# The order of the first mixer in a three-block kernel: projections between the inverse's steps, attention under inverse and scan, and half of its output product in other banks

## The chip, the cores and the metric

The kernel runs on one core of one Trainium2 chip. The metric is device time in microseconds (us); lower is better.

## The reference

The input is 256 tokens of 1024 values, to which 16 meta tokens are added in front. One block with two kinds of mixer comes first, then a layer of differential attention and a layer of stick-breaking attention, each with its MLP. The change touches the first block's mixer alone:

```
u = rms_norm(h, norm_mix_pre)
proj = u @ w_in
dq, dk, dv, dz, db, da, aq, ak, av = split(proj)      # 4 x 512, 8, 8, 512, 128, 128 columns
o_dn = gated_deltanet_group(dq, dk, dv, dz, db, da, conv_w, ...)
o_at = axial_gqa_group(aq, ak, av, q_norm, k_norm)
mix = concat([o_dn, o_at]) @ w_out
h = h + rms_norm(mix, norm_mix_post)

gated_deltanet_group: q, k, v = split(silu(short_conv(concat[dq, dk, dv])))   # 5 taps along the tokens
    q, k = l2_norm(q), l2_norm(k)                     # 4 heads of 128
    per chunk of 64 tokens: uw = triangular_solve(I + A, [v * beta, k * beta * exp(g)]) 
    o = scan over the chunks, once forward and once backward, and their sum
    o = rms_norm(o, o_norm_w) * silu(dz)
axial_gqa_group: rms_norm and rope on q (8 heads of 64) and k (2 heads), softmax(q k^T) v
```

All is computed in float32. A product of an activation with a weight is made of three matmuls of rounded halves: both operands are split into a high and a low part, and low times low is left out.

## The kernel before

**Engines.** Everything is written out by hand: each engine has its own instruction stream and counting semaphores between them. Two lists of steps, `STAGE_1` and `STAGE_2`, give the order of the first mixer. Each engine walks both lists with `in_order`, and runs its own part of each step that it has one for. So moving a name in a list moves the step on TensorE (PE), VectorE (DVE), ScalarE (ACT) and GpSimd (POOL) at once.

**Weights.** SyncE (SP) loads weights in tiles of 1 MB into `RAW`, a ring of three. Each tile holds two halves. ACT writes the high part `WH` of a half (L1219), DVE (L1610) or POOL (L2119, in the first mixer every other half) the low part `WL`. `WH` and `WL` are rings of four halves, and a half is freed once PE has used it. `ahead(n)` is the place in an engine's stream where it splits half n. The three matmuls of `mm3` are L580, L581 and L582. Steps that take a half of weights: `conv.0` to `conv.11` (24 matmuls of 272 columns, 128 channels of dq, dk, dv each), `kv.0` to `kv.3`, `q.0` to `q.4` (with `ba` a few columns at the start), `z.0` to `z.4`, and the output product.

**Steps without weights.** `conv.i`'s taps are four DVE operations (L1731) that read its PSUM bank. `ktok`, `vtok` turn k and v by transposes. `start`, `meta` prepare the chunks. `inv.0` to `inv.14` invert the triangular matrices of all chunks at once; their matmuls are L822, L827 and L832 (128x128), and L842 and L848 (64x64) for `inv.13` and `inv.14`; between two of them stand DVE operations. `solve` (L862) is followed by a chain of small DVE operations (L1828, L1830). `rows.0` to `rows.3` are the norm and the rope of attention's q and k on POOL and DVE. `qp.0` to `qp.2` prepare q for the scan: PE (L929, L937 sums of squares by 128x1 products), DVE (L1879, L1883, L1885), POOL (the square root by a power, L2123), and DVE again (L1918). `in.0`, `in.1` (L949, L959, L960) turn attention's q and k.

**Second list.** `scan.d.i` is step i of the scan in direction d: L974, L988/L989, L996, L1004 and L1012 are its matmuls. `gqa.n` is one of 20 attention pieces: scores of piece n (L1024), the maximum, exponent and reciprocal on DVE and ACT (L1946, L1948, L1953, L1955), transposes of an earlier piece (L1034, L1036), and a product with v of one earlier still (L1045, L1046, L1047). The result goes to `MH`/`ML` 4 to 7. `on.0` to `on.6` are the norm and gate of the scan's result, mostly on POOL (L2292 squares, L2295, L2123 power, L2301, L2304), the transposes (L1059) and `MH`/`ML` 0 to 3. The output product follows: `out_half(n, k)` for k = 0 to 5 (12 matmuls of 512 columns each) and `out_last` for k = 6 and 7, into PSUM banks 0 to 3; then `between` (norm and residual), `features` (transposes into banks 4 to 7) and the MLP. `WROW`, a row buffer, holds z's gate until `on` has used it; then SP loads the norm's row there for `between`.

**PSUM.** Eight banks. The projections use 4 and 5, the inverse 0 to 3, other steps 6 and 7. `keep_warm` (L591) fills PE's pauses at the layer's borders with products that nothing reads.

## Time and profile before

| | us |
|---|---|
| median of 3 runs (lowest to highest) | 1148.88 (1143.24 to 1149.07) |
| profiled execution | 1142.91 |
| its span, from first to last instruction | 1141.1 |
| PE busy in the span | 1077.6 |
| DVE, ACT, POOL busy | 632.9, 555.7, 243.3 |
| mean granted TensorE clock | 0.973 of full |

The profiled execution is one run of its own. Its time stands beside its span, which is 1.8 us shorter, and lies 6.0 us under the median. [...] In the span the first list runs from about 20 to 176 us, the second from 176 to 242 us, the output product from 242 to 263.8 us.

### The profile page before, as it was taken

The page shows a single profiled execution, that of the slowest core. Times are in us where ns is not written, and L with a number is a line of the kernel's source. Part 1 is how long each engine was busy: PE and PEld are TensorE (multiplying, and loading weights), DVE is VectorE, ACT ScalarE, POOL GpSimd, SP SyncE. Part 2 cuts the span into 40 slices and gives each one's busy share as a digit, 9 for nine tenths or more (in the row PEclk, how much of TensorE's full clock was granted, in tenths as well). Part 3 has the DMA queues.
Part 4 walks back from the last instruction along what each step waited for, and adds up shares of the span by engine and source line. Part 5 has one row for each costly group of instructions (what it writes and reads, how often), then busy time and mean ns, then how long its engine had stood idle before and what let it go on. Part 6 is the DMA issues. An engine that isn't in the chain of part 4 may idle for free.

```text
span 1141.1 us, 17631 instructions
## 1 busy us (share of the span) xinstructions
PE 1077.6 (94%) x7367; PEld 966.0 (85%) x7367; DVE 632.9 (55%) x923; ACT 555.7 (49%) x907; POOL 243.3 (21%) x200
## 2 busy tenths in 40 slices
PE   6988998999999999998889999999999999999998
PEld 4977897668999998988668999999899878999997
DVE  4885743636555556167766555546543446554554
ACT  5642332346444545554436444444776656444443
POOL 2522641231000000776351000000332220000000
PEclk8998996999999999999889999999999999999999
DMA  8322200034665565343223565555343324555551
GB/s 256 112 87 98 77 36 0 2 92 134 193 208 184 186 190 198 116 145 121 101 83 125 191 212 185 179 191 186 128 148 111 111 91 146 189 184 187 190 178 73
DMA packets 113951, 160.47 MB, mean 141 GB/s; under 512 B 3776, under 2 KB 97088, under 8 KB 113872
## 3 DMA queue, kind: packets, MB, share of 16 engines
q1 hardware_dynamic: 113872, 159.35, 42.9%
q8 instruction: 58, 0.95, 0.4%
q14 instruction: 21, 0.17, 0.0%
HBM read 158.29 MB, written 1.05 MB: 140 GB/s over the span
## 4 chain that ended last, share of the span: by engine, by line
PE 82%; DVE 9%; ACT 4%; issue 2%; POOL 2%; DMA 0%; SPq 0%; DVEq 0%; POOLq 0%; ACTq 0%
PE PS L580 23%; PE PS L582 22%; PE PS L581 22%; ACT SCR L1219 3%; DVE SCR L1731 1%; PE PS L607 1%; DVE SCR L2048 1%; POOL SM L2123 1%; PE PS L1180 1%; DVE H L1657 1%; PE PS L1203 1%; PE PS L974 1%; PE PS L1104 1%; PE PS L827 1%; PE PS L822 1%
## 5 line engine op out<-in xcount | busy, mean ns | idle before, releaser
L1219 ACT ACTIVATE WH<-RAW 128x1024 fp32r<-128x1024 f32 (+1 forms) x291 | 304.1, 1054 | 247.2 <-PE PS L582 247.0
L1610 DVE TENSOR_TENSOR WL<-RAW,WH 128x1024 fp32r<-128x1024 f32 x226 | 282.9, 1259 | 233.3 <-ACT WH L1219 233.3
L580 PE MATMUL PS<-UH,WH 128*128 128x256 f32 (+2 forms) x1128 | 318.9, 283 | 3.5 <-POOL WL L2119 3.4
L582 PE MATMUL PS<-UH,WL 128*128 128x256 f32 (+2 forms) x1128 | 318.6, 282 | 0.0
L581 PE MATMUL PS<-UL,WH 128*128 128x256 f32 (+2 forms) x1128 | 318.5, 282 | 0.0
L580 PEld LDWEIGHTS PS<-UH,WH 128*128 128x128 f32 (+1 forms) x1128 | 212.4, 188 | 6.6 <-POOL WL L2119 3.5
L581 PEld LDWEIGHTS PS<-UL,WH 128*128 128x128 f32 (+1 forms) x1128 | 211.7, 188 | 1.8
L582 PEld LDWEIGHTS PS<-UH,WL 128*128 128x128 f32 (+1 forms) x1128 | 212.7, 189 | 0.6
L2119 POOL TENSOR_TENSOR WL<-RAW,WH 128x1024 fp32r<-128x1024 f32 (+1 forms) x65 | 155.5, 2402 | 210.6 <-ACT WH L1219 210.6
L580 PE MATMUL PS<-WH,MH 128*128 128x512 f32 (+1 forms) x464 | 177.4, 382 | 5.3 <-DVE ML L2054 3.0
L581 PE MATMUL PS<-WL,MH 128*128 128x512 f32 (+1 forms) x464 | 175.5, 378 | 0.0
L582 PE MATMUL PS<-WH,ML 128*128 128x512 f32 (+1 forms) x464 | 175.0, 377 | 0.0
L1219 ACT ACTIVATE SCR<-PS 128x512 f32<-128x512 f32 (+7 forms) x199 | 95.5, 506 | 150.5 <-PE PS L582 71.2
L2123 POOL TENSOR_TENSOR SM<-SM 128x1 f32<-128x1 f32 (+6 forms) x34 | 30.0, 882 | 590.9 <-DVE SM L1621 577.2
L580 PEld LDWEIGHTS PS<-WH,MH 128*128 128x128 f32 x464 | 88.3, 190 | 22.9 <-issue 8.2
L582 PEld LDWEIGHTS PS<-WH,ML 128*128 128x128 f32 x464 | 88.3, 190 | 16.4
L581 PEld LDWEIGHTS PS<-WL,MH 128*128 128x128 f32 x464 | 88.1, 190 | 14.1
L580 PE MATMUL PS<-WH,UH 128*128 128x256 f32 (+2 forms) x248 | 77.5, 312 | 4.7 <-DVE SCR L1731 4.7
L581 PE MATMUL PS<-WL,UH 128*128 128x256 f32 (+2 forms) x248 | 75.5, 304 | 0.0
L582 PE MATMUL PS<-WH,UL 128*128 128x256 f32 (+2 forms) x248 | 75.3, 304 | 0.0
L580 PEld LDWEIGHTS PS<-WH,UH 128*128 128x128 f32 (+1 forms) x248 | 48.3, 195 | 6.9 <-DVE SCR L1731 4.8
L1219 ACT ACTIVATE MH<-SCR 128x512 fp32r<-128x512 f32 (+1 forms) x41 | 25.2, 616 | 53.8 <-DVE SCR L1677 53.8
(286 smaller groups left out, 1257.3 us busy)
## 6 DMA issues: line engine op xcount, KB each, us to landing
RAW<-in_gu SPq DMA_DIRECT2D x44, 1024.0 KB, 5.1
RAW<-in_dn SPq DMA_DIRECT2D x22, 1024.0 KB, 4.9
RAW<-in_w_up SPq DMA_DIRECT2D x16, 1024.0 KB, 5.8
RAW<-in_w_down SPq DMA_DIRECT2D x16, 1024.0 KB, 4.9
...
```

The lines of the kernel that those rows point to most:

```text
L580: e.matmul(o, lh, rh, start=start, stop=False)
L581: e.matmul(o, lh, rl, start=False, stop=False)
L582: return e.matmul(o, ll, rh, start=False, stop=stop)
L607: ins = e.transpose(PS[:, b, o + 128 * c:o + 128 * c + 128], XN[:, c, 128 * k:128 * k + 128], idn)
L822: ins = e.matmul(v[:, h, :], MT[:, h, :], X[:, h, :], start=True, stop=True)
L827: ins = e.matmul(v[:, h, :], XT[:, h, :], T0[:, h, :], start=True, stop=True)
L974: ins = e.matmul(v0[:, h, :], T0[:, h, :], X[:, h, :], start=True, stop=True)
L1104: ins = e.matmul(PS[:, 4 + i, 0:nk], QTT[64 * i:64 * i + 64, h, 128 * c:128 * c + 128], KTT[64 * i:64 * i + 64, h, 0:nk], start=True, stop ...
L1219: return e.activation(o, i, func, bias=bias, scale=scale, accum_out=acc)
L1610: e.tensor_tensor(half_view(WL, n_), half_src(n_), half_view(WH, n_).bitcast(F32), SUB).then_inc(s_lo_dve, 1)
L2119: e.tensor_tensor(half_view(WL, n_), half_src(n_), half_view(WH, n_).bitcast(F32), SUB).then_inc(s_lo_pool, 1)
L2123: e.tensor_tensor(o, x, s, POW).then_inc(*done)
```

## The change

The diff, cut to its core:

```diff
 STAGE_1 = steps_of(
-    "ba gates.0 conv.0 conv.1 gates.1 conv.2 gates.2 conv.3 gates.3 silu.0 conv.4 conv.5 ktok.0 conv.6 ktok.1 conv.7 "
-    "start.0 start.1 meta.0 silu.1 kv.0 kv.1 inv.0 kv.2 kv.3 inv.1 meta.1 vtok.0 q.0 q.1 solve vtok.1 q.2 q.3 inv.2 "
-    "inv.3 meta.2 vtok.2 q.4 conv.8 inv.4 rows.0 conv.9 inv.5 meta.3 conv.10 inv.6 rows.1 conv.11 silu.2 inv.7 meta.4 "
-    "z.0 z.1 inv.8 rows.2 z.2 z.3 inv.9 meta.5 z.4 rows.3 inv.10 meta.6 inv.11 inv.12 qp.0 inv.13 qp.1 inv.14 qp.2 "
-    "in.0 in.1")
+    "ba gates.0 conv.0 conv.1 gates.1 conv.2 gates.2 conv.3 gates.3 silu.0 kv.0 kv.1 ktok.0 ktok.1 kv.2 kv.3 start.0 start.1 "
+    "meta.0 q.0 q.1 inv.0 meta.1 q.2 inv.1 q.3 q.4 rows.0 z.0 solve z.1 z.2 z.3 z.4 inv.2 inv.3 meta.2 conv.4 inv.4 conv.5 "
+    "inv.5 meta.3 conv.6 inv.6 rows.1 conv.7 silu.1 inv.7 meta.4 conv.8 inv.8 vtok.0 conv.9 inv.9 vtok.1 vtok.2 rows.2 "
+    "meta.5 conv.10 inv.10 meta.6 rows.3 conv.11 silu.2 inv.11 in.0 in.1 inv.12 gqa.0 qp.0 inv.13 gqa.1 qp.1 inv.14 gqa.2 "
+    "qp.2 gqa.3")
 STAGE_2 = steps_of(
-    " ".join(f"scan.0.{i} scan.1.{i} gqa.{i}" for i in range(8)) +
-    " on.0 gqa.8 on.1 gqa.9 on.2 gqa.10 gqa.11 on.3 gqa.12 on.4 gqa.13 gqa.14 gqa.15 gqa.16 gqa.17 on.5 gqa.18 on.6 gqa.19")
+    " ".join(f"scan.0.{i} gqa.{2 * i + 4} scan.1.{i} gqa.{2 * i + 5}" for i in range(8)) +
+    " on.0 og.4 on.1 og.5 on.2 og.6 on.3 og.7 on.4 on.5 on.6")
...
         w_cols("ba", win, 2048, 16)
-        for b in (2, 3, 4, 5):
+        for b in (2, 3):
             w_cols(("conv", b), win, 256 * b, 256)
         w_rows("kv", win, 0, 8, 2576, 256)
         for k in range(2):
             w_rows(("q", k), win, 4 * k, 4, 2064, 512)
-        for b in (0, 1):
-            w_cols(("conv", b), win, 256 * b, 256)
         for k in range(2):
             w_rows(("z", k), win, 4 * k, 4, 1536, 512)
-        for k in range(4):
+        for b in (4, 5, 0, 1):
+            w_cols(("conv", b), win, 256 * b, 256)
+        for k in (2, 3, 0, 1):
             w_rows(("out", 1, k), A["w_out"], 2 * k, 2, 0, 1024)
...
+        QSQ = SCR[:, at[0] - 1024:at[0]].rearrange("p (a b) -> p a b", a=4)
...
-        TA, TB = PB[0][:, 0:256], PB[1][:, 0:256]
+        TA, TB, TK = (O[i // 2].rearrange("p a b -> p (a b)")[:, 256 * (i % 2):256 * (i % 2) + 256] for i in range(3))
...
+        SUMS = [4 if r == 1 else 0 for r in range(7)]
+        TURN = [0 if r == 1 else 4 for r in range(6)]
...
-                return mm3(PS[:, 2 * c + m, :], MH[:, k, t], ML[:, k, t], wh[:, 0, s], wl[:, 0, s], start, stop)
+                return mm3(PS[:, SUMS[r] + 2 * c + m, :], MH[:, k, t], ML[:, k, t], wh[:, 0, s], wl[:, 0, s], start, stop)
...
+            def og(k):
+                out_half(1, half_of(("out", 1, k // 2), k % 2), k, mix_ready(1, k), k == 4)
+
...
-            in_order(STAGE_2, dict(scan=scan, gqa=gqa, on=on))
-            for k in range(6):
-                out_half(half_of(("out", 1, k // 2), k % 2), k, mix_ready(1, k), k == 0)
-            out_last(1, [half_of(("out", 1, 3), j) for j in range(2)], [6, 7], [mix_ready(1, 6), mix_ready(1, 7)])
+            in_order(STAGE_2, dict(scan=scan, gqa=gqa, on=on, og=og))
+            for k in range(2):
+                out_half(1, half_of(("out", 1, 0), k), k, mix_ready(1, k), False)
+            out_last(1, [half_of(("out", 1, 1), j) for j in range(2)], [2, 3], [mix_ready(1, 2), mix_ready(1, 3)])
...
             def gqa_in(i):
                 if i == 0:
-                    ac.wait_ge(*qp_p["n"])
...
-                    dv.wait_ge(*vt_v[2])
...
+            def og(k):
+                ahead(half_of(("out", 1, k // 2), k % 2))
+
...
-                    po.wait_ge(*me_a["s", 1])
-                    e.tensor_tensor(QTG, CV[:, 0:4, 16:272], CV[:, 0:4, 16:272], MUL).then_inc(*qp_o.step("sq"))
+                    po.wait_ge(*gr_v[1, 1, "s2"])
+                    po.wait_ge(*gr_o[1, 1, "s2"])
+                    e.tensor_tensor(QSQ, CV[:, 0:4, 16:272], CV[:, 0:4, 16:272], MUL).then_inc(*qp_o.step("sq"))
```

In words. Of the convolution's projections only dk's four now come ahead of `kv`, `q` and `z`; the other eight stand between the steps of the inverse. Attention begins already in the first list, and its pieces alternate with the scan's steps. The output product begins with attention's own half, k = 4 to 7 (`og`), between the steps of `on`; k = 0 to 3 follow. It sums into banks 4 to 7, and the `features` that follow use banks 0 to 3. The weights come in the order of their new use. Some temporaries have moved to other buffers, so that three waits fall away. PE does the same products as before.

The change adds four lines ahead of `mm3` and some later: L580 to L582 of before are L584 to L586 of the changed kernel, PE's L842, L848, L929, L937, L974, L1024, L1034, L1036 are L846, L852, L933, L941, L978, L1028, L1038, L1040, L988/L989 are L992/L993, DVE's L1879, L1883, L1885, L1918, L1946, L1948, L1953, L1955 are L1887, L1891, L1893, L1925, L1953, L1955, L1960, L1962, and POOL's L2119, L2123, L2292, L2295, L2301, L2304 are L2129, L2133, L2305, L2308, L2314, L2317.

PE's stream from the last inverse steps to the first scan steps, before (L832 is `inv.12`, L929 `qp.0` and `qp.1`, L842 and L848 `inv.13` and `inv.14`, L937 `qp.2`, L949 to L960 `in.0` and `in.1`, L974 the scan, L1024 attention's scores):

```order
L832 MATMUL PS<-CST,SCR 128x128 x16
L929 MATMUL PS<-SCR 128x128 x4
L842 MATMUL PS<-SCR 64x64 x16
L929 MATMUL PS<-SCR 128x128 x4
L848 MATMUL PS<-SCR 64x64 x16
L937 MATMUL PS<-CST,SCR 128x1 x8
L949 MATMUL PS<-CST,SCR 128x128 x8
...
L974 MATMUL PS<-SCR 128x128 x8
L1024 MATMUL PS<-SCR 128x272
L974 MATMUL PS<-SCR 128x128 x8
L1024 MATMUL PS<-SCR 128x272
L988 MATMUL PS<-SCR 128x128
```

The same place in the changed kernel; `in.0` and `in.1` now stand ahead of it:

```order
L836 MATMUL PS<-CST,SCR 128x128 x16
L1028 MATMUL PS<-SCR 128x272
L933 MATMUL PS<-SCR 128x128 x4
L846 MATMUL PS<-SCR 64x64 x16
...
L1028 MATMUL PS<-SCR 128x272
L941 MATMUL PS<-CST,SCR 128x1 x8
L1028 MATMUL PS<-SCR 128x272
L1038 MATMUL PS<-CST,SCR 128x128 x2
L1040 MATMUL PS<-CST,SCR 16x128
L978 MATMUL PS<-SCR 128x128 x4
L1028 MATMUL PS<-SCR 128x272
```

What moved: `in.0` and `in.1` no longer lie between `qp.2` and the scan's first step; two scores (L1028) and the transposes of one piece do, and scores and the scan's products now alternate by four.

DVE's stream at the same place, before (L1879 to L1918 belong to `qp.2` and the scan's first step, L1946 and L1948 to attention):

```order
L1879 TENSOR_SCALAR SM<-PS 128x2x4
L1883 TENSOR_SCALAR SM<-SM 128x2x4
L1885 TENSOR_TENSOR SM<-SM 128x8
L1918 TENSOR_TENSOR SCR<-SCR,SM 128x512
L1946 TENSOR_REDUCE SM<-PS 128x1
```

And in the changed kernel:

```order
L1887 TENSOR_SCALAR SM<-PS 128x2x4
L1891 TENSOR_SCALAR SM<-SM 128x2x4
L1893 TENSOR_TENSOR SM<-SM 128x8
L1953 TENSOR_REDUCE SM<-PS 128x1
L1955 TENSOR_SCALAR SM<-SM 128x1
L1960 RECIPROCAL SM<-SM 128x1
L1962 TENSOR_SCALAR SCR<-SCR,SM 128x272
L1925 TENSOR_TENSOR SCR<-SCR,SM 128x512
```

What moved: four operations of an attention piece now stand between `qp.2`'s last scalar (L1893) and the operand of the scan's first step (L1925).

POOL's stream around `on`, before (L2292 to L2304 are `on`, L2119 the low parts of the output product's and the MLP's weights):

```order
L2292 TENSOR_TENSOR SCR<-SCR 128x512 x2
L2295 TENSOR_SCALAR SM<-SM 128x8
L2123 TENSOR_TENSOR SM<-SM 128x8
L2301 TENSOR_TENSOR SCR<-SCR,SM 128x512
L2304 TENSOR_TENSOR SCR<-SCR,WROW 128x512
L2301 TENSOR_TENSOR SCR<-SCR,SM 128x512
L2304 TENSOR_TENSOR SCR<-SCR,WROW 128x512
L2119 TENSOR_TENSOR WL<-RAW,WH 128x1024 x4
```

And in the changed kernel:

```order
L2305 TENSOR_TENSOR SCR<-SCR 128x512
L2129 TENSOR_TENSOR WL<-RAW,WH 128x1024
L2305 TENSOR_TENSOR SCR<-SCR 128x512
L2308 TENSOR_SCALAR SM<-SM 128x8
L2133 TENSOR_TENSOR SM<-SM 128x8
L2129 TENSOR_TENSOR WL<-RAW,WH 128x1024
L2314 TENSOR_TENSOR SCR<-SCR,SM 128x512
L2317 TENSOR_TENSOR SCR<-SCR,WROW 128x512
L2314 TENSOR_TENSOR SCR<-SCR,SM 128x512
L2317 TENSOR_TENSOR SCR<-SCR,WROW 128x512
```

What moved: two low parts (halves 26 and 28) now stand inside the chain of `on`, where none stood before.

## Rows read from the trace of the kernel before

**Rows 1.** The page: busy time of the engines, share of the span

```profile
PE 1077.6 (94%) x7367; PEld 966.0 (85%) x7367; DVE 632.9 (55%) x923; ACT 555.7 (49%) x907; POOL 243.3 (21%) x200
```

**Rows 2.** Windows (us, busy of PE, PEld, DVE, ACT, POOL, clock, DMA share, GB/s)

```profile
44.00:264.00 220.00, 202.42 (x1324) 167.44 (x1323) 124.17 (x272) 82.69 (x170) 82.23 (x74) 0.92 0.19 61
...
65.00:69.00 4.00, 4.00 (x22) 4.00 (x23) 3.96 (x14) 1.17 (x2) 0.64 (x1) 0.57 0.00 0
...
89.00:96.00 7.00, 4.79 (x14) 3.92 (x15) 2.79 (x10) 0.00 (x0) 0.00 (x0) 0.51 0.43 145
...
167.70:191.60 23.90, 22.18 (x89) 17.52 (x89) 4.95 (x10) 6.71 (x13) 6.18 (x5) 0.50 0.00 0
191.60:242.00 50.40, 45.86 (x259) 29.05 (x258) 30.34 (x93) 16.11 (x51) 11.09 (x10) 1.00 0.03 11
242.00:264.00 22.00, 22.00 (x99) 18.23 (x99) 6.68 (x9) 10.06 (x15) 10.15 (x5) 1.00 0.49 149
```

**Rows 3.** What PE waited for from 44 to 264 us: total, times, longest

```profile
PE PS L580 <- DVE SCR L1731: 4.7, 1, 4.7
PE PS L774 <- DVE SCR L1828: 4.0, 1, 4.0
PE PS L1004 <- DVE SCR L1930: 1.9, 2, 1.0
...
PE PS L974 <- issue: 1.4, 1, 1.4
```

**Rows 4.** PE in order of time, 166 to 192 us: start, us, operation

```profile
166.51 2.52 PE L937 MATMUL PS<-CST,SCR 128*128 128x1 f32 x16
...
182.46 3.76 PE L974 MATMUL PS<-SCR 128*128 128x128 f32 x16 [1.37 <-issue]
...
187.35 0.79 PE L988 MATMUL PS<-SCR 128*128 128x128 f32 x2
```

**Rows 5.** DVE in order of time: a convolution's taps; then 168 to 176 us

```profile
43.14 2.10 DVE L1731 SCALAR_TENSOR_TENSOR SCR<-PS,COLS,SCR 128x270 f32<-128x270 f32 x4 [0.25 <-ACT SCR L1219]
...
169.06 0.17 DVE L1879 TENSOR_SCALAR SM<-PS 128x8 f32<-128x8 f32 x1 [2.98 <-PE PS L937]
170.99 1.00 DVE L1883 TENSOR_SCALAR SM<-SM 128x8 f32<-128x8 f32 x1 [1.76 <-POOL SM L2123]
172.02 0.96 DVE L1885 TENSOR_TENSOR SM<-SM 128x8 f32<-128x8 f32 x1
172.91 0.68 DVE L1918 TENSOR_TENSOR SCR<-SCR,SM 128x512 f32<-128x512 f32 x1
```

**Rows 6.** DVE, one attention piece at 224 us

```profile
223.82 0.44 DVE L1946 TENSOR_REDUCE SM<-PS 128x1 f32<-128x272 f32 x1
...
224.56 0.36 DVE L1955 TENSOR_SCALAR SCR<-SCR,SM 128x272 f32<-128x272 f32 x1
```

**Rows 7.** POOL in order of time: `rows.0`, `qp.2`, `on` and a low part

```profile
113.61 2.91 POOL L2123 TENSOR_TENSOR SM<-SM 128x16 f32<-128x16 f32 x1
...
120.47 2.37 POOL L2119 TENSOR_TENSOR WL<-RAW,WH 128x1024 fp32r<-128x1024 f32 x1
...
169.31 1.65 POOL L2123 TENSOR_TENSOR SM<-SM 128x8 f32<-128x8 f32 x1 [8.01 <-DVE SM L1879]
170.92 1.04 POOL L2281 TENSOR_TENSOR SCR<-SCR,SM 128x512 f32<-128x512 f32 x1
...
216.13 2.10 POOL L2292 TENSOR_TENSOR SCR<-SCR 128x512 f32<-128x512 f32 x2 [1.43 <-DVE SCR L1939]
...
222.77 1.64 POOL L2123 TENSOR_TENSOR SM<-SM 128x8 f32<-128x8 f32 x1
...
227.04 1.04 POOL L2301 TENSOR_TENSOR SCR<-SCR,SM 128x512 f32<-128x512 f32 x1 [2.63 <-DVE SM L1973]
228.16 1.29 POOL L2304 TENSOR_TENSOR SCR<-SCR,WROW 128x512 f32<-128x512 f32 x1
```

**Rows 8.** PE by line, 217 to 234 us, attention alone: busy, mean ns

```profile
L1024 PE MATMUL PS<-SCR 64*128 64x272 f32 x16 | 5.8, 441 | 0.0
```

More of the change, by code:

```diff
@@ L670, in out_last @@
                 for b in range(4):
-                    emptied[b] = mixed[b // 2][r, b % 2]
+                    emptied[SUMS[r] + b] = mixed[b // 2][r, b % 2]
             def mlp(r, u):
@@ L1466, in on @@
                         act(MH[:, h, :], PS[:, h, 0:256], ACT.Copy).then_inc(*mx_hi.step((1, h)))
-            in_order(STAGE_1, dict(ba=ba, gates=gates, conv=conv, silu=silu, kv=kv, q=q, z=z, ktok=ktok, start=start, inv=inv, meta=meta,
+            in_order(STAGE_1, dict(gqa=gqa, ba=ba, gates=gates, conv=conv, silu=silu, kv=kv, q=q, z=z, ktok=ktok, start=start, inv=inv, meta=meta,
                                **{"in": gqa_in}))
-            in_order(STAGE_2, dict(scan=scan, gqa=gqa, on=on))
-            for k in range(7):
+            in_order(STAGE_2, dict(scan=scan, gqa=gqa, on=on, og=og))
+            for k in range(3):
                 ahead(half_of(("out", 1, k // 2), k % 2))
@@ L1960, in gqa, with og @@
                                            ).then_inc(*mg_lo.step(j))
+            def og(k):
+                ahead(half_of(("out", 1, k // 2), k % 2))
             def on(i):
@@ L1978, in on @@
                                                ).then_inc(*mx_lo.step((1, h)))
-            in_order(STAGE_1, dict(ba=ba, gates=gates, conv=conv, kv=kv, q=q, z=z, ktok=ktok, vtok=vtok, start=start, inv=inv, meta=meta,
+            in_order(STAGE_1, dict(gqa=gqa, ba=ba, gates=gates, conv=conv, kv=kv, q=q, z=z, ktok=ktok, vtok=vtok, start=start, inv=inv, meta=meta,
                                solve=solve, qp=qp, rows=rows))
-            in_order(STAGE_2, dict(scan=scan, gqa=gqa, on=on))
-            for k in range(7):
+            in_order(STAGE_2, dict(scan=scan, gqa=gqa, on=on, og=og))
+            for k in range(3):
                 ahead(half_of(("out", 1, k // 2), k % 2))
@@ L2286, in scan, with og @@
                     e.tensor_tensor(O[c], O[c], grp[d, c][4], ADD).then_inc(*sc_o[d].step("o"))
+            def og(k):
+                ahead(half_of(("out", 1, k // 2), k % 2))
             def on(i):
@@ L2306, in _ @@
             in_order(STAGE_1, dict(ba=ba, gates=gates, conv=conv, kv=kv, q=q, z=z, ktok=ktok, meta=meta, qp=qp, rows=rows))
-            in_order(STAGE_2, dict(scan=scan, on=on))
-            ahead(half_of(("out", 1, 3)))
+            in_order(STAGE_2, dict(scan=scan, on=on, og=og))
+            ahead(half_of(("out", 1, 1)))
             between(1)
```

44 lines of the change are left out of this document (21 added, 23 removed).

## The prediction, on record before the changed kernel ran

> **What bounds the kernel now.** I read the page first: PE is busy in 94% of the span, every other engine in 55% or less [rows 1]. So a stretch of the kernel lasts as long as PE's own work at the clock that it is granted, plus what PE waits. The products stay the same, so the change can only move those two. Then I read windows around what moves, 44 to 264 us: PE busy 202.4 of 220 us, clock 0.92 [rows 2]. That leaves two stores:
>
> - Waiting: 220.0 - 202.4 = 17.6 us. The chain of waits names 4.7 us at `kv.0` behind a convolution's taps, 4.0 us at L774 behind the small DVE operations after `solve`, 1.9 us in the scan (twice), 1.4 us at the scan's second step [rows 3]. The rest, 5.6 us, is small.
> - [...] 65 to 69 us, right behind the 4.7 us wait, has a mean of 0.57 over 4 us: about 3.4 us at half, of which half, 1.7 us, is lost. 89 to 96 us, around the 4.0 us wait, has 4.79 us of busy time at 0.51: 2.4 us lost. 167.7 to 191.6 us has 22.18 us of busy time at 0.50: 11.1 us lost [rows 2]. Together 15.2 us.
>
> The third piece has no long wait in front. It begins with the thinnest PE work of the stage, the 64x64 products of `inv.13` and `inv.14` and `qp.2`'s 128x1 products, of which 16 rows take 2.52 us [rows 4]. It ends only inside the unbroken run of L988/L989 that begins at 187.35 us [rows 4].
>
> **The change part by part.** I walked PE's new stream with the durations of before, full clock where it was full.
>
> *Work.* The same products, no term. The output product is 96 matmuls in 21.8 us, whichever banks and order they take; a bank's number has no row of its own and no reason for a price. The loads are the same tiles in another order. DMA's share is 0.19 in this stretch [rows 2], so a tile is there when its half is split.
>
> *Waits that go.* `kv.0` now stands right behind `conv.3`, whose four taps take 2.10 us [rows 5]. From PE's end of `conv.3` to the taps' end 1.15 us stay of 4.7. The chain after `solve` takes 4 us on DVE as before, but `z.1` to `z.4`, 4 x 2.8 us of products, now lie between: the 4.0 us go. The 1.4 us at the scan's second step is replaced below.
>
> *Waits that come.* (1) `z.0` waits some 0.65 us (an estimate, one ACT copy) until `q.4`'s bank is free. (2) `z.3` takes half 14, an even one, whose low part is POOL's, and POOL has `rows.0` in front of it (the norm's square root alone 2.91 us, the low part 2.37 us [rows 7]). By my walk it is ready 2.9 us after PE wants it. (3) By the walk 0.3 us at `inv.3` and 0.9 us at `meta.5` behind `vtok.2`. (4) Ahead of the scan's first step stands what `qp.2` needs: L1879 0.17, POOL's power 1.65, L1883 1.00, L1885 0.96, then four operations of piece 3 that stand between (1.10 us from 223.82 to 224.92 in a piece like it [rows 6]), then L1918 0.68 [rows 5, 7]: 5.6 us. Before, `in.0` and `in.1` lay in between, and L1918, begun at 172.91, was done well before the scan at 176 us. Now two scores and the transposes of one piece lie there, about 1.2 us. PE waits 4.3 us (4.0 to 4.6 by how the ends fall). (5) In the scan 1.9 us as before. (6) Behind the scan POOL is the long pole: squares 2.10, a power of 1.64 with a short scalar ahead, two products per half of 1.04 and 1.29, so 4.7 [rows 7], two low parts that now stand between, 4.8, and 1.7 us for the crossings to DVE and back: 15.1 us from the last attention piece to the gated result. `og.4` to `og.7`, 48 matmuls, cover half of the product's 21.8, 10.9 us. PE waits 4.2 us, and 0.3 for the transposes. Before, twelve attention pieces stood between `on`'s steps and covered this. (7) Small ones I set at 1.2 us, against 5.6 before, since attention and scan now alternate and each has work of the other behind which to hide.
> Sum: 1.15 + 0.65 + 2.9 + 1.2 + 4.3 + 1.9 + 4.5 + 1.2 = 17.8 us, against 17.6. The waits pay nothing, they only change places.
>
> *Clock.* All hangs on it. With no half clock anywhere the stretch would be 15.2 - 0.2 = 15.0 us shorter. But every pause of 4 us or more in this stretch had half clock around it [rows 2, 3]. The new pauses are 2.9 us before `z.3`, 4.3 us before the scan, 4.2 us before the last half of the product. For the first and the last I take what the old ones cost, 1.7 and 2.4, less a little for the shorter one: 1.6 + 2.4 = 4.0 us. For the middle one I take a fall for certain: `inv.13`, `inv.14` and `qp.2` are still there, now with a pause right behind them.
> How long it stays down is the unknown. Bound from below: the old pauses were over after 3.4 and 6.8 us, with dense work behind them. Bound from above: the old third piece lasted 23.9 us, over scan products and scores [rows 2]. Now behind the pause come scan products of four with attention's scores, transposes and products with v between. From 191.6 us on, the same kinds of products held full clock over 50.4 us, though PE waited 4.5 of them [rows 2]. But from 182.46 to 187.35 us scan products and scores at half clock did not raise it, and L988/L989 did [rows 4]. I take 8 us of busy time at half, nearer the short end, since the mix is richer than the one that failed: 4.0 us lost.
>
> [...] At 170.99 us L1883 and L1885, 128x8 elements each, took 1.00 and 0.96 us beside POOL's L2281 of 1.04 us, while L1879 of the same size took 0.17 alone [rows 5, 7]. [...]
>
> **Sum.** Clock and waits -15.0, side pauses +4.0, middle +4.0: -7.0 us. Against the profiled execution that is 1142.9 - 7.0 = 1135.9 us. The runs shown have a median 6.0 us above it, so I say 1148.9 - 7.0 = 1141.9 us. Outside the stretch nothing moves: the norm's row for `between` is loaded when `on` is done with its buffer, and 10.9 us of product lie between.
>
> **The rivals.** A change of under about 0.5%, 5.7 us, can't be told from none.
>
> - A, my forecast (0.40): as summed. By the side pauses (0 to 4 us) and the length at half it lies between -12 and -2 us: 1137 to 1147.
> - B, the clock comes back only in the scan's L988/L989, as before (0.24). Up to those lie 13.1 us of work at full clock, which then cost twice: 32 scan products, 3.8 us (16 took 3.76 at half [rows 4]), and four and a half attention pieces at 2.1 us, 9.3 (two rows of L1024 are a piece, so eight pieces took 17 us [rows 8]). -15.0 + 4.0 + 13.1 = +2: 1151. For it: 182.46 to 187.35 us. Against it: attention's transposes and 256-column products were not in that mix.
> - C, the other side (0.16): attention now also splits the run of L988/L989 in groups of eight, so the very thing that raised the clock is gone, and half clock goes on into the rest of the second list. Of the 45.9 us that PE was busy from 191.6 to 242 us [rows 2] some 10 are done by then, so 36 us are left; half to most of it slow, 17 to 30 us, gives, with B's +2, +19 to +32: 1168 to 1181. It decides if 8 us or more of work behind the first L992 still run at half. Against it: 191.6 to 242 us at full clock with waits [rows 2]. For it: that stretch never had to climb, it only had to stay up.
> - D, no fall in the middle and none at the sides (0.10): the scores among `inv.12` to `qp.2` make that place dense enough. -15.0: 1134. Against it the pause of 4.3 us.
> - E, a wait that I don't see (0.10): low parts, loads or ring slots that come late because an engine's order now puts them behind something, such as (2) or (6) longer by 5 us or more. With A that gives about -2 to +8, say 1152.
>
> **How the numbers follow.** The likeliest is A, 1141.9 us. The range 1132 to 1163 takes in A, B, D and E and leaves out C, 0.16, and a few hundredths below D. Signs are mixed: A's own range is 1137 to 1147. Faster by over 0.5%: A 0.27, D 0.10, B 0.03, in all 0.40. Within 0.5%: A 0.13, B 0.14, E 0.06, in all 0.33. Slower: B 0.07, C 0.16, E 0.04, in all 0.27.
>
> **What would show it.** In the profile after: PE's waits at `kv.0` about 1 us, none at L774 after `solve`, one near 3 us in the `z` steps on POOL's low part, one near 4 us on L1925 before the first L978, one near 4 us between `og.7` and the transposes of `on`. Windows from the pause on show how long 0.50 lasts: some 8 us is A, until the first L992 is B, far past it C, none is D. I would be wrong if the pause before the scan were under 2 us (then D), if the half clock began already in the `inv` steps and went through to the scan, or if the wait for `on` were 8 us or more, because the two low parts come late from SP's loads.

## The result, and the profile after

The changed kernel takes 1157.33 us (median of 4 runs, 1155.65 to 1157.61), the kernel before, timed beside it, 1148.95 us. The ratio is 1.0085 with a 95% interval of 1.0057 to 1.0114: slower, by 8.4 us in the medians. Forecast were 1141.9 us and a gain. The time lies inside the stated range of 1132 to 1163 us, but on the other side of the kernel before. The profiled execution took 1157.22 us, 14.3 us more than that of before. The kernel before has executions near 1143.5 and near 1148.8 us, and its profile is one of the first kind; the median beside the changed kernel, 1148.95 us, comes from three of the second kind and one of the first. In the later timings most were of the first kind (medians of 1143.7 to 1144.5 us), so the loss is nearer 13 us against those.

The page and windows over the stretch that the change touches, to compare with [rows 1, 2] (columns as there). The first window is the stretch, the others are those in which the profile grants half clock, 0.50 of full:

```profile
PE 1085.7 (94%) x7367; PEld 971.7 (84%) x7367; DVE 649.2 (56%) x923; ACT 555.2 (48%) x907; POOL 244.6 (21%) x200
```

```profile
44.00:280.00 236.00, 211.67 (x1333) 174.04 (x1332) 141.70 (x273) 83.23 (x172) 83.62 (x74) 0.88 0.18 58
79.30:86.10 6.80, 6.80 (x28) 6.22 (x28) 2.54 (x7) 0.00 (x0) 5.08 (x5) 0.50 0.01 2
96.40:103.20 6.80, 6.24 (x33) 5.46 (x34) 3.08 (x5) 3.48 (x6) 1.57 (x2) 0.50 0.24 85
144.20:147.60 3.40, 3.40 (x16) 3.40 (x17) 3.33 (x7) 0.00 (x0) 3.17 (x6) 0.50 0.51 133
178.30:209.00 30.70, 25.25 (x81) 16.53 (x81) 9.63 (x26) 6.83 (x19) 4.76 (x5) 0.50 0.00 1
263.60:270.50 6.90, 6.22 (x18) 5.13 (x19) 1.70 (x4) 2.48 (x5) 3.00 (x2) 0.51 0.24 77
```

PE is idle for 236.0 - 211.7 = 24.3 us, against 17.6. It is busy at half clock for 47.9 us, so half clock costs 24.0 us, against 15.2. Together 15.5 us more. The output product ends at 278.96 us, before at 263.84: 15.1 us later. So the whole loss lies in this stretch, to within 0.8 us at the end of the span, and it is 6.7 us of waiting and 8.8 us of clock.

What PE waited for there, to compare with [rows 3]:

```profile
PE PS L978 <- DVE SCR L1925: 5.6, 1, 5.6
PE PS L1063 <- POOL SCR L2317: 5.5, 2, 3.5
PE PS L817 <- DVE SCR L1817: 3.8, 2, 3.2
PE PS L866 <- DVE SCR L1812: 2.9, 1, 2.9
PE PS L1008 <- DVE SCR L1937: 1.8, 2, 0.9
PE PS L913 <- DVE SCR L1780: 1.3, 1, 1.3
```

The old waits of 4.7 and 4.0 us are gone. In their place stand one before the scan's first step (L978), one before `on`'s transposes (L1063), and two in the inverse: `solve` (L866) and `inv.3` (L817).

PE around the scan's start, in order of time, to compare with [rows 4]:

```profile
177.92 0.27 PE L1040 MATMUL PS<-CST,SCR 128*16 128x128 f32 x1
183.75 2.05 PE L978 MATMUL PS<-SCR 128*128 128x128 f32 x8 [5.56 <-DVE SCR L1925]
...
205.16 0.80 PE L992 MATMUL PS<-SCR 128*128 128x128 f32 x2
...
209.96 0.39 PE L992 MATMUL PS<-SCR 128*128 128x128 f32 x2
```

The clock falls at 178.3 us. The wait has then lasted 0.1 us (L1040 ends at 178.19), so it is not the wait that brought the clock down. Ahead of it stand `inv.13`, `inv.14` and `qp.2`'s 128x1 products. Eight rows of scan products then take 2.05 us, not the 1.06 us that they take at full clock (e5). The clock comes back only inside the first unbroken run of L992/L993, at 209.0 us: two rows of them take 0.80 us at 205.16 and 0.39 us at 209.96.

DVE's chain ahead of the scan, against [rows 5], and three places before it:

```profile
65.53 4.70 DVE L1854 TENSOR_TENSOR SCR<-SCR,CST 16x64 f32<-16x64 f32 x1 [0.37 <-POOL SCR L2222]
...
70.40 0.20 DVE L1854 TENSOR_TENSOR SCR<-SCR,CST 16x64 f32<-16x64 f32 x1
...
87.02 2.05 DVE L1838 TENSOR_TENSOR SCR<-SCR 128x96 f32<-128x96 f32 x1
...
94.59 4.62 DVE L1817 TENSOR_TENSOR SCR<-SCR,CST 128x512 f32<-128x512 f32 x4
...
177.10 0.17 DVE L1887 TENSOR_SCALAR SM<-PS 128x8 f32<-128x8 f32 x1 [0.78 <-PE PS L941]
179.03 1.00 DVE L1891 TENSOR_SCALAR SM<-SM 128x8 f32<-128x8 f32 x1 [1.76 <-POOL SM L2133]
...
182.08 1.52 DVE L1925 TENSOR_TENSOR SCR<-SCR,SM 128x512 f32<-128x512 f32 x1
```

POOL at the same times, against [rows 7]:

```profile
65.40 4.75 POOL L2129 TENSOR_TENSOR WL<-RAW,WH 128x1024 fp32r<-128x1024 f32 x2
...
86.52 4.80 POOL L2129 TENSOR_TENSOR WL<-RAW,WH 128x1024 fp32r<-128x1024 f32 x2
...
93.90 3.56 POOL L2207 TENSOR_TENSOR WROW<-WROW,ROWS 128x512 f32<-128x512 f32 x2 [2.58 <-ACT WROW L1226]
```

L1854 reads 16x64 elements. It takes 0.20 us alone and 4.70 us when it meets two low parts of POOL in a row that last 4.75 together. L1838 on 128x96 takes 2.05 us next to a low part; the same operation takes 0.26 us next to nothing in the kernel before, where it is L1830. The four L1817 take 4.62 us, against 2.49 in the kernel before; what runs beside them is L2207, not a low part.

### The profile page after: what moved, and what is told of

Its sections match the earlier page's. It is cut to its first block, busy times and chain, and to the rows that moved or that the text cites. A ratio compares the mean times of both kernels' runs of the same rounds, so it can differ in the third digit from the quotient of the medians.

```text
span 1155.4 us, 17635 instructions
## 1 busy us (share of the span) xinstructions
PE 1085.7 (94%) x7367; PEld 971.7 (84%) x7367; DVE 649.2 (56%) x923; ACT 555.2 (48%) x907; POOL 244.6 (21%) x200
## 4 chain that ended last, share of the span: by engine, by line
PE 79%; DVE 10%; ACT 4%; issue 3%; POOL 3%; DMA 0%; SPq 0%; DVEq 0%; POOLq 0%; ACTq 0%
PE PS L584 22%; PE PS L586 21%; PE PS L585 21%; ACT SCR L1226 3%; POOL SM L2133 1%; PE PS L611 1%; DVE SCR L2058 1%; PE PS L826 1%; PE PS L1187 1%; PE PS L1028 1%; POOL WL L2129 1%; DVE H L1665 1%; DVE SCR L1739 1%; PE PS L1210 1%; PE PS L978 1%
## 5 line engine op out<-in xcount | busy, mean ns | idle before, releaser
L584 PE MATMUL PS<-UH,WH 128*128 128x256 f32 (+2 forms) x1128 | 320.3, 284 | 3.5 <-POOL WL L2129 3.4
L586 PE MATMUL PS<-UH,WL 128*128 128x256 f32 (+2 forms) x1128 | 319.8, 284 | 0.0
L584 PEld LDWEIGHTS PS<-UH,WH 128*128 128x128 f32 (+1 forms) x1128 | 213.6, 189 | 6.3 <-POOL WL L2129 3.5
L586 PEld LDWEIGHTS PS<-UH,WL 128*128 128x128 f32 (+1 forms) x1128 | 213.8, 190 | 0.6
L2129 POOL TENSOR_TENSOR WL<-RAW,WH 128x1024 fp32r<-128x1024 f32 (+1 forms) x65 | 155.1, 2397 | 194.1 <-ACT WH L1226 194.1
L584 PE MATMUL PS<-WH,MH 128*128 128x512 f32 (+1 forms) x464 | 178.7, 385 | 5.3 <-DVE ML L2064 3.0
L586 PE MATMUL PS<-WH,ML 128*128 128x512 f32 (+1 forms) x464 | 175.5, 378 | 0.0
L1226 ACT ACTIVATE SCR<-PS 128x512 f32<-128x512 f32 (+8 forms) x199 | 95.2, 507 | 160.6 <-PE PS L586 72.8
L2133 POOL TENSOR_TENSOR SM<-SM 128x1 f32<-128x1 f32 (+6 forms) x34 | 30.0, 883 | 596.1 <-DVE SM L1629 576.9
L584 PEld LDWEIGHTS PS<-WH,MH 128*128 128x128 f32 x464 | 88.7, 191 | 23.1 <-issue 8.2
L586 PEld LDWEIGHTS PS<-WH,ML 128*128 128x128 f32 x464 | 88.6, 191 | 16.7
L584 PE MATMUL PS<-WH,UH 128*128 128x256 f32 (+2 forms) x248 | 76.2, 307 | 1.8 <-DVE SCR L1739 1.0
L586 PE MATMUL PS<-WH,UL 128*128 128x256 f32 (+2 forms) x248 | 74.1, 299 | 0.0
L584 PEld LDWEIGHTS PS<-WH,UH 128*128 128x128 f32 (+1 forms) x248 | 47.2, 190 | 4.4 <-issue 1.5
```

Of the source, the lines that this page charges most:

```text
L584: e.matmul(o, lh, rh, start=start, stop=False)
L586: return e.matmul(o, ll, rh, start=False, stop=stop)
L1226: return e.activation(o, i, func, bias=bias, scale=scale, accum_out=acc)
L2129: e.tensor_tensor(half_view(WL, n_), half_src(n_), half_view(WH, n_).bitcast(F32), SUB).then_inc(s_lo_pool, 1)
L2133: e.tensor_tensor(o, x, s, POW).then_inc(*done)
```

## The experiments

The experiments change the order of steps, who makes a low part, or add warming products (`keep_warm`, read by nobody; "filler" below) where PE waits. "Idle" and "lost" are sums over PE's stretch from 44 us to the end of the output product, from the profiled execution of each run. "Lost" is half of PE's busy time at half clock.

| kernel | median us | ratio to before, 95% | product ends | idle | lost |
|---|---|---|---|---|---|
| before | 1148.95 | | 263.8 | 17.6 | 15.2 |
| changed | 1157.33 | 1.0057 to 1.0114 | 279.0 | 24.3 | 24.0 |
| e1 `qp` early | 1157.43 | 1.0044 to 1.0129 | 269.8 | 19.8 | 19.6 |
| e2 44 warming products | 1153.15 | 1.0043 to 1.0103 | 271.8 | 17.9 | 12.8 |
| e3 low parts of `on` by DVE | 1155.69 | 1.0054 to 1.0108 | 276.8 | 22.5 | 22.6 |
| e4 low parts of q, z by DVE | 1154.02 | 1.0018 to 1.0094 | 278.3 | 22.2 | 24.8 |
| e5 20 warming products | 1144.22 | 0.9987 to 1.0031 | 268.0 | 18.9 | 12.0 |
| e6 projections' order alone | 1145.40 | 0.9993 to 1.0043 | 265.4 | 14.8 | 19.9 |
| e7 attention under `on` | 1154.43 | 1.0051 to 1.0156 | 277.2 | 21.9 | 24.2 |
| e8 three edits | 1142.59 | 0.9962 to 1.0040 | 264.3 | 15.0 | 13.3 |
| e9 before, 12 warming products | 1146.85 | 1.0013 to 1.0034 | 265.6 | 17.1 | 14.5 |
| e10 e8 and two more fillers | 1138.96 | 0.9933 to 0.9967 | 260.6 | 11.2 | 6.8 |
| e11 e8 with `qp` early | 1146.93 | 1.0002 to 1.0033 | 268.3 | 18.7 | 15.9 |

The kernel before was timed anew beside each group: 1144.49 us for e1 to e4, 1144.05 for e5 to e8, 1143.70 for e9 to e11. Its executions lie in separate groups, and the ratio is not simply the quotient of two medians. Besides the two groups named above, five of its 71 later executions took 1132.3 to 1133.3 us, at a mean clock of 0.981 to 0.983 instead of 0.971. That is 11 us less, which is what its half clock from 167.7 to 191.6 us costs (11.1 us); no trace of such an execution was kept, so where their clock stayed up is not shown. The changed kernel was timed in the first round alone, in four executions, so "under the changed kernel" compares two rounds of timing; the kernel before has its groups at the same times in all of them.

Warming products count as busy, so they are not in "idle"; the part of them at half clock is in "lost".

**e1: does the wait before the scan bring the clock down?**

```diff
-    "... in.0 in.1 inv.12 gqa.0 qp.0 inv.13 gqa.1 qp.1 inv.14 gqa.2 qp.2 gqa.3"
+    "... in.0 in.1 inv.12 qp.0 qp.1 qp.2 gqa.0 inv.13 gqa.1 inv.14 gqa.2 gqa.3"
```

> The changed kernel with qp.0, qp.1 and qp.2 ahead of inv.13, so that DVE and POOL prepare the scan's operand under inv.13, inv.14 and attention pieces 0 to 3. Both theories: PE's wait of 5.6 us for L1925 before the scan shrinks to 1 us or less. Theory pause (the wait makes the clock fall): the half clock from 178 to 209 us is gone or short, so 5 us of wait and 8 to 12 us of clock come off: about 13 to 17 us under the changed kernel, near 1142. Rival thin products (inv.13, inv.14 and qp.2 make it fall whether PE waits or not, as at 167.7 us in the kernel before, which had no wait): half clock still begins near 175 to 180 us and lasts until the scan's L992, only about 4 to 6 us come off, near 1152.

The wait shrank to 0.85 us as expected. The clock fell all the same. PE in order of time:

```profile
169.21 2.13 PE L941 MATMUL PS<-CST,SCR 128*128 128x1 f32 x16 [0.58 <-DVE SCR L1884]
...
176.90 3.30 PE L852 MATMUL PS<-SCR 64*64 64x64 f32 x32
...
184.70 2.05 PE L978 MATMUL PS<-SCR 128*128 128x128 f32 x8 [0.85 <-DVE SCR L1925]
...
187.88 0.69 PE L1038 MATMUL PS<-CST,SCR 128*128 128x128 f32 x2
...
191.46 0.44 PE L1038 MATMUL PS<-CST,SCR 128*128 128x128 f32 x2
...
199.33 0.49 PE L992 MATMUL PS<-SCR 128*128 128x128 f32 x2
```

`inv.14` took 3.30 us, against 1.90 in the changed kernel: half clock began at 170.8 us, in `qp.2`, with no wait ahead of it longer than 0.58 us. It ended at 191.2 us, eight microseconds ahead of the first L992, after 6.5 us of scan products and scores (L1038 takes 0.69 us before and 0.44 us after). So half clock need not last until the L992. The ten executions fall into two groups, four at 1146 to 1150 us and six at 1157 to 1160. The profile is of the first group; the six have a lower mean clock (0.961 to 0.963 against 0.968 to 0.974), and where they lose it is not shown. The rival is right on the fall, which here had thin products and no wait longer than 0.58 us ahead of it, but not on its end. The theory that the wait makes the clock fall fell.

**e2 and e5: the wait stays, but PE has something to do in it.** e2 has 44 for the 20.

```diff
                 if i < 2:
...
+                    if (d, i) == (0, 0):
+                        keep_warm(20, b0)
                     pe.wait_ge(*(sc_o[1] if d else sc_v[0])["t", i])
```

> The changed kernel with 44 warming products (128x128, read by nobody) into bank 0 ahead of the scan's first step, where PE waits 5.6 us; the wait for L1925 itself stays. Theory pause: PE stays busy there, the clock stays at 1.00 until the on steps, 25.3 us of busy time at half become 12.6: about 12 us under the changed kernel, near 1145. Rival thin products: the clock falls anyway before or in the filler, which then takes up to 10 us: same or up to 5 us slower than the changed kernel, 1157 to 1162.

> As the run with 44 warming products ahead of the scan's first step, with 20 instead. There the 44 took 11.6 us, since each leaves two rows of 0.13 us, so they outlasted the 5.6 us wait by 6 us; 20 take about 5.3 us. Theory pause: half clock there is 3 to 7 us long at most instead of 31, and PE loses nothing to the filler: 9 to 12 us under the changed kernel, near 1147. Rival (it was the sheer length of the 44 that brought the clock back, 20 are too few): half clock lasts until the scan's L992 as in the changed kernel, and the time is 1156 to 1158.

e2 took the half clock from 30.7 to 3.4 us (177.3 to 180.7). But 44 products leave 88 rows in the trace, and they lasted 11.62 us, 6 us past the wait. I had sized them by a row each. Its time, 4.2 us under the changed kernel, lies between the two forecasts. e5 in order of time, and its windows after the filler's start:

```profile
179.32 6.26 PE L595 MATMUL PS<-CST 128*128 128x128 f32 x40
185.42 1.06 PE L980 MATMUL PS<-SCR 128*128 128x128 f32 x8
```

```profile
179.70:183.20 3.50, 3.50 (x20) 3.50 (x19) 2.78 (x6) 0.00 (x0) 3.50 (x4) 0.51 0.00 0
183.20:251.40 68.20, 62.44 (x362) 44.64 (x361) 39.09 (x87) 21.14 (x54) 15.03 (x12) 1.00 0.08 21
```

The clock fell although PE had no pause any more, 0.4 us into the filler, and was back 3.4 us later; then 68 us of the very mix of scan and attention ran at full clock. All ten executions lie between 1143.0 and 1145.9 us, 13.1 us under the changed kernel by the medians, by one edit in one place. So the mix can hold full clock. Climbing to it is less sure: in the changed kernel 21 us of the mix, from 183.75 us to the first L992, did not do it, in e1 6.5 us did.

**e3 and e7: the wait for `on`.** e3 takes POOL's two low parts out of the chain, e7 puts attention over it.

```diff
-            on_pool.append(bool(share) and n % share == 0)
+            on_pool.append(bool(share) and n % share == 0 and n not in (26, 28))
```

> The changed kernel with the low parts of halves 26 and 28, which stand inside POOL's chain of on, made by DVE. POOL's chain gets 4.8 us shorter, DVE gets 2.4 us more. Theory port and queue (the two low parts delay the gated result, by their own length and by holding up L1979 and L1983 2.35 us each): PE's waits for L2317, 5.5 us together, fall to 1 us or less, and the half clock from 263.6 to 270.5 us goes: 5 to 9 us under the changed kernel, near 1150. Rival (DVE takes over the delay, since it also has the row sums of on): the wait moves to a DVE line and less than 2 us come off.

```diff
-    " ".join(f"scan.0.{i} gqa.{2 * i + 4} scan.1.{i} gqa.{2 * i + 5}" for i in range(8)) +
-    " on.0 og.4 on.1 og.5 on.2 og.6 on.3 og.7 on.4 on.5 on.6")
+    " ".join(f"scan.0.{i} gqa.{2 * i + 4} scan.1.{i} gqa.{2 * i + 5}" for i in range(6)) +
+    " scan.0.6 gqa.16 scan.1.6 scan.0.7 scan.1.7 on.0 gqa.17 on.1 gqa.18 on.2 gqa.19 og.4 on.3 og.5 og.6 on.4 og.7 on.5 on.6")
```

> The changed kernel with attention pieces 17 to 19 behind on.0, on.1 and on.2, ahead of og.4, so that on's POOL chain starts earlier against PE's work: 5 to 6 us of attention now lie under it. Theory (PE waits since only 10.9 us of product cover a chain of over 15 us): the waits for L2317, 5.5 us, fall to 1 us or less and the half clock of 6.8 us there goes: 5 to 8 us under the changed kernel, near 1151. Rival (DVE and ACT do these pieces late, and POOL waits for DVE's sums behind them): the chain ends later by as much, less than 2 us come off.

e3: the wait for L2317 fell from 5.5 to 3.1 us and the half clock there from 6.9 to 3.4 us, 1.6 us by the medians. e7: 5.5 to 1.3 us, but its half clock of 6.8 us stayed (now at 247.5), 2.9 us by the medians. e7's theory is right on the wait and wrong on the clock. e3's, 1 us or less of wait and 5 to 9 us of time, is wrong in size on both; its rival's "less than 2 us" fits, though no wait moved to a DVE line. The chain in the changed kernel and in e3, DVE in order of time:

```profile
248.90 2.35 DVE L1979 TENSOR_TENSOR SM<-SM 128x4 f32<-128x4 f32 x1
...
256.17 2.35 DVE L1983 TENSOR_TENSOR SM<-SM 128x4 f32<-128x4 f32 x1 [2.05 <-POOL SM L2133]
```

```profile
251.58 0.17 DVE L1979 TENSOR_TENSOR SM<-SM 128x4 f32<-128x4 f32 x1
...
256.55 0.17 DVE L1983 TENSOR_TENSOR SM<-SM 128x4 f32<-128x4 f32 x1 [0.19 <-POOL SM L2133]
```

Four elements a row take 2.35 us beside a low part of POOL (2.39 us) and 0.17 us without. The other direction is there too, in e3: POOL's L2317, 1.26 us by itself, began 0.01 us after a low part of DVE of 1.23 us and took 2.35.

```profile
257.92 2.35 POOL L2317 TENSOR_TENSOR SCR<-SCR,WROW 128x512 f32<-128x512 f32 x1
```

So e3 took 4.8 us out of POOL's chain and gave some of it back.

**e4: the same for q's and z's low parts.** The edit is e3's with the set (8, 10, 12, 14).

> The changed kernel with the low parts of halves 8, 10, 12 and 14 (q's and z's) made by DVE instead of POOL. Theory port (DVE operations with two SBUF inputs are held up for the length of POOL's low part): L1854 (16x64, 4.70 us) and the two L1838 of 2.05 us fall to about 0.3 us, DVE is 8 us less held up and 5 us more busy; the wait of 2.9 us before solve and some of the 3.8 us before inv.2's transposes go, and with them half clock at 79 and 96 us: 3 to 9 us under the changed kernel. Rival (these lengths are not from POOL): L1854 and L1838 stay as long, DVE has 5 us more in a stretch where it is busy 98%, and the kernel gets 2 to 5 us slower.

```profile
67.44 0.21 DVE L1854 TENSOR_TENSOR SCR<-SCR,CST 16x64 f32<-16x64 f32 x1 [0.37 <-POOL SCR L2222]
...
88.89 2.05 DVE L1838 TENSOR_TENSOR SCR<-SCR 128x48 f32<-128x48 f32 x1
```

L1854 fell from 4.70 to 0.21 us and the wait before `solve` from 2.9 to 0.7 us; one L1838 still met a low part, of half 16. The wait at `inv.3` stayed (3.6 us for 3.8), with the four L1817 still at 4.64 us beside L2207. The time didn't follow clearly: idle 2.2 us less, lost 0.8 us more, and of the six executions three took 1147.2 to 1151.5 us and three, the profiled one among them, 1156.6 to 1158.5. So it is shown that POOL's operation holds up DVE's; what that is worth to the whole kernel is not.

**e6: the projections' new order alone.** The first list ends as before, the second is the old one, and the product stands whole behind it.

```diff
-    "... silu.2 inv.11 in.0 in.1 inv.12 gqa.0 qp.0 inv.13 gqa.1 qp.1 inv.14 gqa.2 qp.2 gqa.3"
+    "... silu.2 inv.11 inv.12 qp.0 inv.13 qp.1 inv.14 qp.2 in.0 in.1"
...
-    " ".join(f"scan.0.{i} gqa.{2 * i + 4} scan.1.{i} gqa.{2 * i + 5}" for i in range(8)) +
-    " on.0 og.4 on.1 og.5 on.2 og.6 on.3 og.7 on.4 on.5 on.6")
+    " ".join(f"scan.0.{i} scan.1.{i} gqa.{i}" for i in range(8)) +
+    " on.0 gqa.8 on.1 gqa.9 on.2 gqa.10 gqa.11 on.3 gqa.12 on.4 gqa.13 gqa.14 gqa.15 gqa.16 gqa.17 on.5 gqa.18 on.6 gqa.19"
+    " og.4 og.5 og.6 og.7")
```

> One part of the change alone: the projections between the inverse's steps (and the new load order and buffers), but attention after the inverse and in the old second list, in.0 and in.1 behind qp.2 again, and the whole output product behind the last attention piece, in banks 4 to 7. Theory (attention's new place and the early half of the product cost the time, the projections' order nothing or a little): no wait for L1925 before the scan, none for L2317, half clock near 168 to 192 us as in the kernel before, so 13 to 16 us under the changed kernel, 1141 to 1146, level with before. Rival (the projections' new order costs by itself: waits of 2.9 and 3.8 us at solve and inv.2 and their half clock): 1148 to 1153.

1145.40 us, 11.9 us under the changed kernel and level with before (ratio 0.9993 to 1.0043), as the theory had it. Idle time is 2.8 us less than before, 14.8, and the clock takes it back, 19.9 us lost. Attention's new place and the early half of the product cost the rest; the two are not told apart. Where the clock went I had not foreseen: 3.4 us behind `qp.2`, then 20.5 us in the middle of attention, with one wait of 0.42 us at its start. The first of these ended in `in.0` and `in.1`, the very products over which the kernel before stayed at half clock.

```profile
170.90:174.30 3.40, 3.40 (x14) 2.23 (x14) 1.85 (x2) 1.19 (x2) 3.40 (x3) 0.50 0.00 0
222.10:242.60 20.50, 19.32 (x52) 8.72 (x51) 6.02 (x21) 5.85 (x19) 3.31 (x3) 0.50 0.00 0
```

**e8, e10 and e11: together.** e8 is e5, e7 and e3 in one. e10 adds a filler in each of the two waits in the inverse. e11 is e8 with e1's order and 12 warming products behind `qp.2`, none before the scan.

```diff
             def solve():
...
+                keep_warm(12, 6)
                 for m in iv_v:
                     pe.wait_ge(*m["nc"])
...
                     if i == 3:
+                        if j == 0:
+                            keep_warm(13, 0)
                         pe.wait_ge(*V["e"])
```

> Three edits together: 20 warming products ahead of the scan's first step, attention pieces 17 to 19 under on, and the low parts of halves 26 and 28 made by DVE. If each takes away its own wait and its own half clock, they add up: 10 + 6 us under the changed kernel, 1140 to 1143, at or a little under the kernel before. If a clock that is saved in one place is lost in the next (the short filler leaves it down, or the clock falls elsewhere), 1147 to 1152.

> The combined kernel (20 warming products before the scan, pieces 17 to 19 under on, low parts 26 and 28 by DVE) with 12 warming products more in the 2.9 us wait ahead of solve and 13 in the 3.2 us wait ahead of inv.3. Theory pause for the sides too (half clock at 80 to 87 and 97 to 104 us comes from these waits, 6.5 us lost): 4 to 6 us under the combined kernel, near 1137, under the kernel before. Rival (the clock falls there by the thin work around it, 16x16 products and solve's, filler or not, and the filler outlasts the waits): the same as the combined kernel or up to 4 us slower.

> The combined kernel without the 20 warming products before the scan, but with qp.0, qp.1 and qp.2 ahead of inv.13, and 12 warming products right behind qp.2's. The wait for L1925 (5.6 us) is then hidden under real work, and the filler answers the thin products. Theory: if dense products hold the clock over inv.13 and inv.14, 3 us of wait less the filler's 3: 1 to 4 us under the combined kernel. Rival (inv.13, inv.14 and four scores behind the filler are thin enough to let it fall again, as in the run with qp.2 early): half clock of some 20 us until L992, 5 to 12 us above the combined kernel, and two groups of times.

e8: 1142.59 us, inside the forecast for edits that add up, but only 1.6 us under e5: 14.7 us under the changed kernel, where the three gave 17.6 us one by one. e10: 1138.96 us, ratio 0.9933 to 0.9967: a little faster than the kernel before, and 18.4 us under the changed one. All its executions lie above the five of 1132 to 1133 us that the kernel before had in other rounds. It is 3.6 us under e8, with 4 to 6 forecast. Its windows with half clock, and a wait that is new:

```profile
90.10:93.50 3.40, 3.40 (x10) 2.63 (x9) 3.26 (x6) 0.00 (x0) 1.65 (x1) 0.50 0.88 285
175.40:178.90 3.50, 3.50 (x19) 3.50 (x18) 2.75 (x6) 0.00 (x0) 3.50 (x4) 0.51 0.02 5
233.50:240.30 6.80, 6.80 (x17) 4.77 (x17) 1.72 (x3) 1.48 (x3) 3.62 (x3) 0.50 0.26 58
```

```profile
PE PS L584 <- POOL WL L2134: 1.9, 1, 1.9
```

The two pieces of half clock at 80 and 97 us, 13.6 us in e8, are gone, and so is that at 145 us; one of 3.4 us is new, behind the new wait. So at 80 and 97 us filler in the wait did keep the clock up.

e11: 1146.93 us, 4.3 us above e8. Half clock began at 171.5 us with the filler, and full clock held from 174.9 to 185.2 us, over `inv.13` and `inv.14`. But the filler's 4.47 us stood outside a wait, and 2.2 us of the wait before the scan were left: on DVE L1926, the L1925 of this kernel, stands behind the last two attention pieces and began only at 185.44, 11 us after `qp.2`'s last scalar. At 185.2 us the clock fell again. It was back at 192.0 us, again in the mix and 8.5 us ahead of the first L993, the L992 of this kernel. The rival was nearer on the time, but its 20 us of half clock and its two groups of times did not come. PE and DVE in e11, in order of time:

```profile
189.44 0.69 PE L1039 MATMUL PS<-CST,SCR 128*128 128x128 f32 x2
...
191.98 0.72 PE L1029 MATMUL PS<-SCR 64*128 64x272 f32 x2
```

```profile
173.76 0.17 DVE L1892 TENSOR_SCALAR SM<-SM 128x8 f32<-128x8 f32 x1 [1.76 <-POOL SM L2134]
173.97 0.17 DVE L1894 TENSOR_TENSOR SM<-SM 128x8 f32<-128x8 f32 x1
```

The last two are the L1891 and L1893 of the changed kernel. POOL had nothing beside them here, and they took 0.17 us each, not 1.00 and 0.96.

**e9: the same filler in the kernel before**, ahead of its scan, 12 products.

> The kernel before with 12 warming products (24 rows) ahead of the scan's first step, where it has no wait but half clock since 167.7 us, until the dense L988/L989 raise it at 191.6. Theory (dense 128x128 products in one run raise the clock, wherever they stand): the filler takes 3 to 5.6 us, the clock is back at the latest 7 us after it begins, and 7 to 8 us of the 11.1 that half clock costs come back: 2 to 5 us under the kernel before in the executions in which the clock had fallen. Rival (only a pause's end lets the clock rise, or the scan's thin mix takes it down again at once): 3 to 6 us slower than the kernel before.

```profile
176.59 5.43 PE L591 MATMUL PS<-CST 128*128 128x128 f32 x24
...
188.43 0.49 PE L990 MATMUL PS<-SCR 128*128 128x128 f32 x2
...
192.85 1.16 PE L998 MATMUL PS<-SCR 128*128 128x128 f32 x8
```

The same products as that last row, in the kernel before:

```profile
193.78 1.16 PE L996 MATMUL PS<-SCR 128*128 128x128 f32 x8
```

The clock was back at 181.8 us, 5.2 us into the filler and 10 us earlier than before, so here dense products did raise it. The filler stood in no wait and took 5.43 us, and the clock gave more than that back: at L998 PE was 0.9 us ahead of the kernel before. Then 6.8 us of half clock appeared at 236.5 us, where the kernel before had none, and at the product's end PE was 1.8 us behind. 1146.85 us, 2.3 per mille over before, within 2 us in all twelve executions. The theory's 2 to 5 us of gain did not come, and the loss does not lie where the filler stands. The rival's 3 to 6 us of loss fits the time, but not its mechanism: the clock did rise on filler without a pause, and the scan did not take it down again. Whether the filler brought about the later fall is not shown; e6 lost the clock in the same part of attention without any filler.

## Why the prediction was wrong

The waits were sought in the right places, and the place of the risk, the clock behind the wait before the scan, was named. The step that failed is the choice of its length: "I take 8 us of busy time at half, nearer the short end, since the mix is richer than the one that failed: 4.0 us lost". It was 25.3 us, 12.6 lost. That is rival B's mechanism (0.24): half clock until the scan's L992. Its price, 13.1 us, was right within a microsecond; its time, 1151 us, was not, since the side pauses and the waits came on top. The evidence for it was the row at hand, scan products and scores that had not raised the clock from 182 to 187 us. I weighed against it that the same mix had held full clock later. e5 shows that the mix holds full clock for 68 us, the changed kernel that it need not climb to it in 21 us. Nor is the opposite a rule: in e1 and e11 the same mix did climb, 6.5 and 5.7 us after the scan's start. So 8 us was not an impossible length; what was missing was a reason to put it before 25 us, and the only row that I had on climbing spoke for the long one. The prediction also took the fall for a matter of the pause in part. The fall comes 0.1 us into the pause, and in e1 and e5 without one; what lay ahead of it each time was `qp.2` and its surroundings, which it named too.

Point by point, in the terms of the sum:

- Side pauses, "1.6 + 2.4 = 4.0 us": 11.3 us, from four pieces (6.8 + 6.2 + 3.4 + 6.2 of busy time). The second cause of the miss, 7.3 us. The pieces at 79 and 96 us stand at waits that I had at zero and at 0.3, and went in e10 with filler in those waits. That at 144 us stands behind 16x16 products and a wait of 1.3 us.
- Waits, 17.8 us forecast, 24.3 measured. `kv.0` 1.0 for 1.15, scan 1.8 for 1.9, `meta.5` 1.3 for 0.9, an ACT copy at `z.0` 0.8 for 0.65: right.
- Wait (2), 2.9 us at `z.3` behind POOL's low part: not there. PE came late to it by then, through the wait at `solve` and half clock. In e10, where both are gone, it is there with 1.9 us.
- Wait at `solve`, none forecast, 2.9 us; wait at `inv.3`, 0.3 forecast, 3.8 us. Both end on DVE, and DVE was held up: L1854 by 4.5 us, two L1838 by 1.8 each, four L1817 by some 2 us together. e4 shows it for the first wait, which fell to 0.7 us; for the second it is argued. The prediction had a first sign of it, L1883 and L1885 at 1.00 and 0.96 us beside POOL's L2281, and its sum has no term for it. The traces show how long such operations, with two SBUF inputs, were held up, L1854 for 4.70 us beside 4.75 of POOL and L1979 for 2.35 beside 2.39; what inside the chip does it is not shown. The other direction occurs too, with L2314 of `on` at 1.96 us for 1.04 beside a low part of DVE, and L2317 in e3 at 2.35 for 1.26. What cost more is the first one, POOL's operations holding up small DVE operations that PE waits for. The trace of before had a row of it, this one beside a low part of POOL of 2.39 us from 69.11 us on, where the like operation before it took 0.67 us:

```profile
70.00 2.05 DVE L1801 TENSOR_TENSOR SCR<-SCR,CST 128x512 f32<-128x512 f32 x1
```

- Wait (4), 4.3 forecast, 5.6 measured. The durations were near those in [rows 5, 6] but for L1925, 1.52 us for 0.68, beside POOL's product of 1.10 us.
- Wait (6), 4.5 forecast, 5.5 measured: L1979 and L1983 took 2.35 us each beside the two low parts. The 1.7 us for the crossings to DVE and back were my estimate, with no row behind it. In e3, where POOL has no low part in the chain, it was 1.0 us from L1976's start to POOL's L2308 and 0.3 us from the end of the power to L2314.
- "Outside the stretch nothing moves": right within 0.8 us (15.1 us later at the end of the product, 14.3 at the end of the span).
- "6.0 us above it": this was added to the profile's time since the median of before lay in the group near 1148.8 us. The changed kernel shows no such pair of groups; its four executions lie within 2 us. So the median missed by 15.4 us where the sum of its terms missed by 22.4, and 6.0 us of the difference are luck.

With all the errors in, 8.6 for the middle piece (12.6 for 4.0), 7.3 for the side pauses and 6.5 for the waits, -7.0 + 8.6 + 7.3 + 6.5 = +15.4 us against 15.1 measured at the product's end. What stays open: why the mix climbed in e1 and e11 and not in the changed kernel, what splits e1, e4 and the kernel before into groups of times, and why e6 and e9 lost the clock at 222 and 236 us. The runs show that the work around is thin there, not what decides in one execution and not in the next.
